# The gated short convolution of layer 1 moved into the slabs of its own input projection

## What is computed

```python
def short_conv_mix(h, conv_prefix, w_in, w_conv, w_out):
    gate_b, gate_c, xp = jnp.split(h @ w_in, 3, axis=-1)
    u = gate_c * xp
    u_ext = jnp.concatenate([conv_prefix.astype(u.dtype), u], axis=1)
    t = h.shape[1]
    y = w_conv[0] * u_ext[:, 0:t]
    for i in range(1, CONV_WIDTH):
        y = y + w_conv[i] * u_ext[:, i:i + t]
    return (gate_b * y) @ w_out, u_ext[:, -(CONV_WIDTH - 1):]
```

## Time and profile before

| | us |
|---|---|
| median of 3 runs | 3022.16 |
| lowest, highest run | 3018.03, 3022.17 |
| the profiled execution's own time | 3018.97 |
| its span (first to last instruction) | 3016.9 |
| PE busy in the span | 2865.7 (95%) |
| DVE, ACT, POOL busy | 1274.5, 860.5, 273.9 |

### The profile page before, as it was taken

How to read it: one execution, slowest core, us unless ns; L and a number is a source line. 1 busy time by engine, 2 the same in 40 slices (tenths; PEclk the granted TensorE clock), 3 DMA queues, 4 the chain that set the end, 5 groups by cost and what they waited for, 6 DMA issues and landing times.

```text
span 3016.9 us, 49528 instructions
## 1 busy us (share of the span) xinstructions
PE 2865.7 (95%) x21191; PEld 2776.5 (92%) x21191; DVE 1274.5 (42%) x1612; ACT 860.5 (29%) x891; POOL 273.9 (9%) x238
## 2 busy tenths in 40 slices
PE   6999999999996799999998689999999999999998
PEld 5987999999996799999998679999999878999997
DVE  3346543333435343334346654333343365433333
ACT  3136432222211232223223233122231264322222
POOL 5000100000104200000102620000010000000001
PEclk8999999999997899999999779999999999999999
DMA  3210232222221222222221012222222101322221
GB/s 122 87 65 1 80 109 82 84 84 84 84 84 42 56 84 84 84 84 70 85 70 64 1 42 84 84 84 84 81 96 77 53 32 60 113 84 84 84 84 46
DMA packets 205445, 223.38 MB, mean 74 GB/s; under 512 B 3734, under 2 KB 200416, under 8 KB 205312
## 3 DMA queue, kind: packets, MB, share of 16 engines
q1 hardware_dynamic: 200336, 203.70, 21.1%
q0 software_dynamic: 4976, 17.74, 1.8%
HBM read 208.56 MB, written 12.86 MB: 73 GB/s over the span
## 4 chain that ended last, share of the span: by engine, by line
PE 77%; issue 15%; DVE 3%; ACT 2%; POOL 2%; DMA 1%; POOLq 0%; DVEq 0%; ACTq 0%
PE bank L340 67%; PE bank L446 4%; PE bank L420 2%; PE bank L589 1%; POOL big L1420 1%; ACT big L795 1%; PE bank L477 1%; DMA out<-mixs 1%; PE bank L413 0%; PE bank L634 0%; DVE mixs L1128 0%; PE bank L631 0%; PE bank L643 0%; DVE stg L1221 0%; DVE stg L1248 0%
## 5 line engine op out<-in xcount | busy, mean ns | idle before, releaser
L340 PE MATMUL bank<-ahi,whi 128*128 128x288 f32 x3584 | 770.1, 297 | 7.0 <-DVE alo L1003 6.5
L340 PE MATMUL bank<-alo,whi 128*128 128x288 f32 x3584 | 767.4, 296 | 0.0
L340 PE MATMUL bank<-ahi,wlo 128*128 128x288 f32 x3584 | 767.1, 296 | 0.0
L682 ACT ACTIVATE whi<-raw 128x2048 fp32r<-128x2048 f32 x191 | 365.0, 1911 | 897.5 <-PE bank L340 877.6
L340 PE MATMUL bank<-hhi,whi 128*128 128x288 f32 x2560 | 556.6, 299 | 54.2 <-DVE hlo L1138 39.7
L340 PEld LDWEIGHTS bank<-ahi,whi 128*128 128x128 f32 x3584 | 578.5, 189 | 9.9 <-DVE wlo L976 7.4
L340 PEld LDWEIGHTS bank<-alo,whi 128*128 128x128 f32 x3584 | 578.2, 189 | 0.0
L340 PEld LDWEIGHTS bank<-ahi,wlo 128*128 128x128 f32 x3584 | 577.9, 189 | 0.0
L340 PE MATMUL bank<-hlo,whi 128*128 128x288 f32 x2560 | 553.2, 298 | 0.0
L340 PE MATMUL bank<-hhi,wlo 128*128 128x288 f32 x2560 | 553.2, 298 | 0.0
L976 DVE TENSOR_TENSOR wlo<-raw,whi 128x2048 fp32r<-128x2048 f32 x192 | 440.2, 2293 | 261.5 <-ACT whi L682 259.5
(11 more groups left out here) (250 smaller groups left out, 1787.4 us busy)
## 6 DMA issues: line engine op xcount, KB each, us to landing
raw<-in_mlp_w_up SPq DMA_DIRECT2D x64, 1024.0 KB, 5.3
raw<-in_mlp_w_down SPq DMA_DIRECT2D x64, 1024.0 KB, 5.1
raw<-in_sb_w_qkv SPq DMA_DIRECT2D x24, 1024.0 KB, 5.2
raw<-in_conv_w_in SPq DMA_DIRECT2D x12, 1024.0 KB, 5.2
raw<-in_gla_w_in SPq DMA_DIRECT2D x12, 1024.0 KB, 5.3
raw<-in_sb_w_o SPq DMA_DIRECT2D x8, 1024.0 KB, 5.3
out<-mixs POOLq DMA_DIRECT2D x3, 2048.0 KB, 7.7
out<-big POOLq DMA_DIRECT2D x2, 2048.0 KB, 8.4
```

The costliest lines, as they stand in the source:

```text
L340: mm = pe.matmul(acc[h][:, 0:HALF], w[:, u, k, m * P:(m + 1) * P], a[:, k, h * HALF:(h + 1) * HALF], start=(k == 0 and w is whi and a is a ...
L682: act.activation(whi[:, 1 - u], raw[:, 1 - u], ACT.Copy).then_inc(w_hi, 1)
```

## The change

Four things change, all in layer 1.

The order of the slabs. `in_chunk` and SP's loads take them in groups of three: columns of gate_c, then of xp, then of gate_b, for two chunks of channels at a time. So slabs 0, 1, 2 give chunks 8, 9, then 16, 17, then 0, 1 of `big`; four such groups make the 12 slabs.

The place of the convolution. GpSimd makes u of chunk c as soon as its xp chunk has been evacuated (slab 3i + 1). VectorE makes the taps of the even chunk behind slab 3i + 1, those of the odd one behind chunk m = 0 of slab 3i + 2 (`taps`), and the product with gate_b itself, in place in `big`, behind each chunk of slab 3i + 2. ScalarE's copy follows, and `lo_part` a chunk later, the last one at once. The third tap is written as two instructions (512 and 64 frames) over the xp chunk.

The buffers. `U` becomes two tiles of 580 frames in `e2` (made larger), `Y` one tile `conv_y`; `Gt` is gone. GpSimd copies the last two frames of each u to a new tile `tails`, which the four stores read after the last chunk. The two prefixes of the sample are copied chunk by chunk.

The wait of ScalarE for the four stores is gone. `run` has its slabs of layer 1 written out instead of looped on ScalarE and VectorE.

```diff
@@ -111,7 +111,9 @@
         rt, rt_m, rt_l = (sb(n, [P, NT], F32) for n in ("rt", "rt_m", "rt_l"))
-        e2 = sb("e2", [P, D], F32)
+        e2 = sb("e2", [P, 2 * 580], F32)
+        conv_y = sb("conv_y", [P, 578], F32)
+        tails = sb("tails", [P, 2, 2, KC], F32)
         split_r = passing("split_r", [P, 4 * D], F32R)
@@ -234,10 +236,8 @@
-        U = mixs[:, 0:KC * 580].rearrange("p (c t) -> p c t", c=KC)
-        Y = [mixs[:, 4640 + 580 * i:4640 + 580 * i + 578] for i in range(2)]
-        Gt = [mixs[:, 5800 + 576 * i:5800 + 576 * i + 576] for i in range(2)]
+        U = [e2[:, 580 * i:580 * i + 580] for i in range(2)]
+        prompt, sample = slice(0, TP), slice(TP, T)
@@ -276,6 +276,8 @@
+            if layer == 1:
+                return (8, 16, 0)[s % 3] + 2 * (s // 3) + m
             return (2 * s + m + 16) % 24 if layer == 2 else 2 * s + m
@@ -301,6 +303,11 @@
                     load(base + OUT_SLABS, mix_in[layer][:, :, 0:2 * D], IN_SLABS - OUT_SLABS)
+                elif layer == 1:
+                    for s in range(IN_SLABS):
+                        col = P * in_chunk(layer, s, 0)
+                        sp.wait_ge(w_lo, base + s + 1)
+                        sp.dma_start(raw[:, s % 2], mix_in[layer][:, :, col:col + SLAB]).then_inc(slab_in[s % 2], 16)
                 else:
@@ -827,11 +834,11 @@
-            def convolution(layer):
-                for c in range(KC):
+            def convolution(s, m):
+                if s % 3 == 2:
+                    c = 2 * (s // 3) + m
                     act.wait_ge(g_ready, c + 1)
-                    act.activation(hhi[:, c, :], Gt[c % 2], ACT.Copy).then_inc(mix_hi, 1)
-                act.wait_ge(stored, 16 * 4)
+                    act.activation(hhi[:, c, :], big[:, c, :], ACT.Copy).then_inc(mix_hi, 1)
@@ -917,9 +924,12 @@
                 base = first_slab(layer)
-                run(base, IN_SLABS, nothing, norm=2 * layer, beside=linear_gates if layer == 2 else None)
-                (stick_breaking if layer in (0, 3) else convolution if layer == 1 else linear_attention)(
-                    *((layer, layer // 3) if layer in (0, 3) else (layer,)))
+                run(base, IN_SLABS, nothing, norm=2 * layer, beside=linear_gates if layer == 2 else None,
+                    between=convolution if layer == 1 else None)
+                if layer in (0, 3):
+                    stick_breaking(layer, layer // 3)
+                elif layer == 2:
+                    linear_attention(layer)
@@ -1118,20 +1128,35 @@
-            def convolution(layer):
-                for c in range(KC):
-                    y = Y[c % 2]
-                    w = [vec[:, V_CONV + 8 * i + c:V_CONV + 8 * i + c + 1] for i in range(3)]
-                    dve.wait_ge(u_ready, c + 1)
-                    if c >= 2:
-                        dve.wait_ge(g_ready, c - 1)
-                    dve.tensor_scalar(y, U[:, c, 0:578], w[0], None, ALU.mult).then_inc(y_ready, 1)
-                    for i in (1, 2):
-                        dve.wait_ge(y_ready, 3 * c + i)
-                        dve.scalar_tensor_tensor(y, U[:, c, i:578 + i], w[i], y, ALU.mult, ALU.add).then_inc(y_ready, 1)
-                    if c:
-                        lo_part(layer, c - 1, Gt[(c - 1) % 2])
-                lo_part(layer, KC - 1, Gt[(KC - 1) % 2])
+            def taps(c):
+                w = [vec[:, V_CONV + 8 * i + c:V_CONV + 8 * i + c + 1] for i in range(3)]
+                u, y = U[c % 2], big[:, 16 + c, :]
+                dve.wait_ge(u_ready, c + 1)
+                dve.tensor_scalar(conv_y[:], u[:, 0:578], w[0], None, ALU.mult).then_inc(y_ready, 1)
+                dve.wait_ge(y_ready, 3 * c + 1)
+                dve.scalar_tensor_tensor(conv_y[:], u[:, 1:579], w[1], conv_y[:], ALU.mult, ALU.add).then_inc(y_ready, 1)
+                dve.wait_ge(y_ready, 3 * c + 2)
+                dve.scalar_tensor_tensor(y[:, prompt], u[:, 2:514], w[2], conv_y[:, 0:TP], ALU.mult, ALU.add)
+                dve.scalar_tensor_tensor(y[:, sample], u[:, 516:580], w[2], conv_y[:, 514:578], ALU.mult,
+                                         ALU.add).then_inc(y_ready, 1)
+            def convolution(s, m):
+                c = 2 * (s // 3) + m
+                if s % 3 == 0 and s and m == 0:
+                    lo_part(1, c - 1, big[:, c - 1, :])
+                elif s % 3 == 1 and m == 1:
+                    taps(c - 1)
+                elif s % 3 == 2:
+                    dve.wait_ge(acc_free, 2 * (first_slab(1) + s) + m + 5)
+                    dve.wait_ge(y_ready, 3 * c + 3)
+                    dve.tensor_tensor(big[:, c, :], big[:, c, :], big[:, 16 + c, :], ALU.mult).then_inc(g_ready, 1)
+                    if m == 0:
+                        taps(c + 1)
+                    else:
+                        lo_part(1, c - 1, big[:, c - 1, :])
+                    if c == KC - 1:
+                        lo_part(1, c, big[:, c, :])
@@ -1299,12 +1324,10 @@
                 run(base, IN_SLABS, project_out(layer), norm=2 * layer, beside=linear_gates if layer == 2 else None,
-                    unrolled=layer in (0, 3))
+                    between=convolution if layer == 1 else None, unrolled=layer in (0, 3))
                 if layer in (0, 3):
                     stick_breaking(layer, layer // 3)
-                elif layer == 1:
-                    convolution(layer)
-                else:
+                elif layer == 2:
                     linear_attention(layer)
@@ -1450,35 +1473,29 @@
                 pool.dma_start(sb_k_p[sb_index, 0].rearrange("(t p) h d -> p t (h d)", p=P), KT).then_inc(kv_stored, 16)
-                pool.dma_start(sb_k_s[sb_index, 0].rearrange("p h d -> p (h d)"), e2[0:TS, :]).then_inc(kv_stored, 16)
+                pool.dma_start(sb_k_s[sb_index, 0].rearrange("p h d -> p (h d)"), e2[0:TS, 0:D]).then_inc(kv_stored, 16)
             def convolution(layer):
-                pool.wait_ge(chunk_done, 2 * (first_slab(layer) + IN_SLABS) + 3)
-                pool.memset(U[:, :, 0:2], 0.0)
-                made(pool.tensor_copy(U[:, :, 514:516],
-                                      vec[:, V_STATE:V_STATE + 16].rearrange("p (i c) -> p c i", i=2)))
-                pool.wait_ge(acc_free, 2 * (first_slab(layer) + IN_SLABS) + 4)
-                def gate(c):
-                    g, y = Gt[c % 2], Y[c % 2]
-                    pool.wait_ge(y_ready, 3 * c + 3)
+                state = vec[:, V_STATE:V_STATE + 16].rearrange("p (i c) -> p c i", i=2)
+                pool.wait_ge(kv_stored, 16 * 4)
+                for i in range(2):
+                    made(pool.memset(U[i][:, 0:2], 0.0))
+                for c in range(KC):
+                    u = U[c % 2]
+                    pool.wait_ge(acc_free, 2 * (first_slab(layer) + 3 * (c // 2) + 1) + c % 2 + 5)
                     if c >= 2:
-                        pool.wait_ge(mix_ready, 8 * layer + c - 1)
-                    pool.tensor_tensor(g[:, 0:TP], y[:, 0:TP], big[:, c, 0:TP], ALU.mult)
-                    pool.tensor_tensor(g[:, TP:T], y[:, 514:578], big[:, c, TP:T], ALU.mult).then_inc(g_ready, 1)
-                for c in range(KC):
-                    pool.tensor_tensor(U[:, c, 2:514], big[:, 8 + c, 0:TP], big[:, 16 + c, 0:TP], ALU.mult)
-                    pool.tensor_tensor(U[:, c, 516:580], big[:, 8 + c, TP:T], big[:, 16 + c, TP:T],
+                        pool.wait_ge(y_ready, 3 * (c - 1))
+                    pool.tensor_copy(u[:, 514:516], state[:, c, :])
+                    pool.tensor_tensor(u[:, 2:514], big[:, 8 + c, prompt], big[:, 16 + c, prompt], ALU.mult)
+                    pool.tensor_tensor(u[:, 516:580], big[:, 8 + c, sample], big[:, 16 + c, sample],
                                        ALU.mult).then_inc(u_ready, 1)
-                    if c:
-                        gate(c - 1)
-                gate(KC - 1)
-                pool.wait_ge(u_ready, KC)
+                    pool.wait_ge(u_ready, c + 1)
+                    pool.tensor_copy(tails[:, 0, :, c], u[:, 512:514])
+                    made(pool.tensor_copy(tails[:, 1, :, c], u[:, 578:580]))
                 for i in range(2):
-                    for dst, at_ in ((conv_p, 512), (conv_s, 578)):
+                    for j, dst in ((0, conv_p), (1, conv_s)):
                         pool.dma_start(dst[0, 0, i].rearrange("(c p) -> p c", p=P).unsqueeze(2),
-                                       U[:, :, at_ + i:at_ + i + 1], allow_slow_non_contiguous=True).then_inc(stored, 16)
+                                       tails[:, j, i, :].unsqueeze(2), allow_slow_non_contiguous=True).then_inc(stored, 16)
```

More of the change, by code:

```diff
@@ L209, in weighted @@
         def weighted(u):
-            e = stg[:, (u + 1) * D:(u + 2) * D] if u < 3 else e2[:, :] if u % 5 == 4 else scr[:, u % 5 * D:(u % 5 + 1) * D]
+            e = stg[:, (u + 1) * D:(u + 2) * D] if u < 3 else e2[:, 0:D] if u % 5 == 4 else scr[:, u % 5 * D:(u % 5 + 1) * D]
```

## The result

| kernel | median us | runs, us | against before, 95% interval |
|---|---|---|---|
| before | 3021.33 | 3018.03 to 3022.17 (4) | |
| changed | 2975.06 | 2968.80 to 2976.70 (4) | 0.9851 (0.9838 to 0.9863) |

The change makes the kernel 1.5% faster, 46.3 us. The forecast was 2966.5 us, 55.54 us of gain, and the range ended at 2972: the direction was right, the time lies outside the range, and 8.6 us of the forecast median are missing.

The account below looks back on a forecast made before the run. TensorE's matmuls were taken to bound layer 1 except between input and output projection. Four terms there sum to 55.54 us; 3022.16 - 55.54 = 2966.6, rounded to 2966.5 us, range 2961 to 2972.

Parts of the forecast that it names:

- the four terms of the gain: Layer 1's turn to output projection: 10.83 us before the first matmul, 27.90 starved chunks, 14.54 behind stores, 2.27 slow start.
- the cover in the input projection: VectorE's added convolution work fits beside TensorE: 19.7 to 26.6 us of each 38.40 us group, costing zero.
- The rival of the port: Input projection: GpSimd holds VectorE up and TensorE stops, 0 to 12 us, most likely 4, giving 2970.6; chance 0.10.
- the tail: After the last input chunk: final `hlo` at about 3.6 us, needed at 5.6; cost zero, range 0 to 1.4 us.
- nobody waits for them until the end of the kernel: GpSimd's four stores (3.60 us of issuing) land beside the last slab and output projection, with no one waiting.
- one pace: TensorE's chunk of 48 matmuls costs 6.40 us wherever it runs unbroken, from 409.57 us for 64 chunks.

Follow-up runs that it names:

- the two traces at 6.24: The changed kernel with its four stores left out (median 2953.77 us), and with them written in pieces of 32 bytes (2960.44 us); layer 1 norm to norm 200.79 us in both.
- the second trace: The changed kernel profiled once more with no edit: median 2970.11 us, 0.9850 of before, layer 1 norm to norm 217.55 us.
- spread stores: The changed kernel with its four stores issued singly, two slabs apart, in layer 1's MLP: medians 2953.38 and, run again, 2950.67 us (0.9793 and 0.9775 of before).
- two stores: The changed kernel with two of its four stores left out: median 2964.09 us, 0.9815 of before, layer 1 norm to norm 206.23 us.

## Why the prediction was right and wrong

**Right: the four terms of the gain.** Waiting before the first matmul, starved chunks, ScalarE behind the stores, slow clock: all 55.54 us went. The two kernels that leave out nothing and only move the stores give 205.72 to 205.75 us in four traces against 205.76. That it fits to 0.04 us is in part luck: in these four traces layer 1 ran at 6.40 us a chunk, as the sum assumed; the two traces at 6.24 give 200.79.

**Right: the cover in the input projection, though the slow tap was another.** VectorE was busy 78.27 of 147.30 us, 20.4 per group of three slabs, near the least of the 19.7 to 26.6 forecast. With GpSimd at work the taps took 0.51, 1.88, 0.75 and 0.28 us, 3.4 in all against the 4.1 to 5.4 forecast. The first, which I took for the exposed one (1.53), was fast in all eight chunks; the second was slow in four of the eight, beyond the 1.28 I had as its dear value. With GpSimd idle they took 0.52, 0.82, 0.75 and 0.28. I had also misread one of the earlier trace rows: the tap of 0.52 us at 951.97 was not alone, a product of GpSimd began beside it at 952.13. It had only started first.

```profile
936.38 0.51 DVE L1136 TENSOR_SCALAR conv_y<-e,vec 128x578 f32<-128x578 f32 x1
936.93 1.88 DVE L1138 SCALAR_TENSOR_TENSOR conv_y<-e,vec,conv_y 128x578 f32<-128x578 f32 x1
938.84 0.75 DVE L1140 SCALAR_TENSOR_TENSOR big<-e,vec,conv_y 128x512 f32<-128x512 f32 x1
939.51 0.28 DVE L1141 SCALAR_TENSOR_TENSOR big<-e,vec,conv_y 128x64 f32<-128x64 f32 x1
939.70 2.28 DVE L986 TENSOR_TENSOR wlo<-raw,whi 128x2048 fp32r<-128x2048 f32 x1
942.04 0.82 DVE L1067 TENSOR_TENSOR big<-bank,rstd 128x288 f32<-128x288 f32 x2
...
949.30 0.76 DVE L1153 TENSOR_TENSOR big<-big 128x576 f32<-128x576 f32 x1
949.97 1.60 DVE L1163 TENSOR_TENSOR hlo<-big,hhi 128x576 fp32r<-128x576 f32 x2
```

The evacuation behind taps and split started at 942.04, 0.17 us after its chunk's end (941.87, one chunk before 948.27), which is no delay at all. The rival of the port cost nothing. The rule of the Trainium skill that the prediction cites ("SBUF — State Buffer", "Who interferes with whom") agrees with these rows: the first tap had ended when GpSimd's product began (936.89, 1.30 us), and the second, with two inputs in SBUF, began 0.04 us behind that product and took 1.88 us instead of 0.82.

**Right: the tail.** The last two `hlo` end at 951.57, 3.3 us after the last chunk (948.27, the evacuation's start less 0.17); 3.6 were forecast, and TensorE needed them at 5.6.

**Wrong: "nobody waits for them until the end of the kernel".** This is the step that failed. I moved the four stores from a place where no weight load was in flight (DMA share 0.06 in the earlier trace rows) to one just ahead of a load: GpSimd issues them at 940.13, SP the load of output slab 2 at 942.16. I looked for who waits for the stores, and found nobody. I did not ask what they slow down. The one sentence of the prediction on that load has it start later and has ScalarE read it a whole slab later still; it says nothing of the load's length, usually 5.2 us, and it was 32.8. The rows were there: 17.71 us until the last of four stores of 4 KB had landed meant that something else than bytes takes the time, and the kernel before hid that by standing still. The cost is the 6.08 us of idle and 34.11 - 32.00 = 2.11 us of slow clock after it, 8.19 in all, and 55.54 - 8.19 = 47.35 against the measured 47.37. In the second trace the same step costs 9.70 us of idle and 2.12 of slow clock. None of my rivals had a late load in it.

The Trainium skill ("DMA: Bandwidth & Descriptors", "Queues, rings and completion order") says that each DMA engine takes turns between its queues by whole packets. The trace shows that the two queues share, and not how: the engines moved some 25 GB/s in the middle of the collision, and over 300 where the load ran alone (GB/s in 40 slices, 940 to 985 us of the changed kernel, then 936 to 975 us of the one without stores).

```profile
GB/s 0 4 10 7 0 54 31 23 25 25 25 25 19 18 29 21 35 23 30 119 324 167 33 15 14 25 51 39 38 49 57 98 190 186 56 28 159 374 367 32
```

```profile
GB/s 0 0 0 0 21 309 379 337 29 0 0 0 0 0 0 0 17 68 294 377 299 36 1 0 0 0 0 0 0 0 99 209 381 355 32 0 0 0 0 0
```

The time shows up in the load's own packets: the packets of the same three loads took 62.5% of 45 us on 16 engines (450 us) in the changed kernel and 25.6% of 39 us (160 us) without stores, while the stores' own took 2.6% of the 45 (19 us). Whether a load's packet stands there waiting for its turn, and what a turn of 4-byte pieces lasts, no run here shows.

**Wrong as well: one pace.** "6.40 us wherever TensorE runs unbroken" came from the long stretches. The kernel before has one at 6.29 on average, layer 0's input projection (144.66 us for 23 chunks, against 147.19, with a granted clock of 0.95 in its first 21.6 us), and I had not looked at it. So the range was too narrow on the low side too: the kernels without the gap have medians of 2951 to 2966, and the forecast of 2966.5 would have stood at their upper edge even without the collision. The rival I held likeliest, VectorE held up by GpSimd, had its middle at 2970.6, near the measured time, for a wrong reason.

## What to carry to other kernels

When a wait for a transfer is removed or a transfer is moved, ask not only who waits for it but which transfers it will now share the DMA engines with, and price it by its pieces: 16 KB in pieces of 4 bytes delayed a 1 MB load by 28 to 31 us, 4 KB by 10. Send such a store where no load is needed soon, one at a time with room between, or make its runs longer where the layout allows it. And when the end of a chain is taken away, look up each resource that stood idle during it, since the next wait comes from what will now be busy there.

## What was not expected of the hardware

**TensorE has two paces at full clock.** Between two norms, where it runs unbroken, a chunk takes 6.40 us or 6.24 on average over the whole stretch, at a granted clock of 1.00 in both cases. The chains of the changed kernel and of the one with spread stores, for the same 64 chunks of layer 1's MLP:

```profile
1015.16 409.57 PE bank L347 x3072
```

```profile
1007.51 399.50 PE bank L347 x3072
```

That is 10 us on one MLP, 5 us on layer 1 (204.78 or 199.82 us for 32 chunks). Which pace a stretch gets changes between executions of the same kernel: layer 2's MLP was slow in the changed kernel's first profile (409.56) and fast in its second (399.50), layer 3's input projection fast in the first (143.67 for 23 chunks) and slow in the second (147.21). It is not wholly a lottery: layer 1's MLP was fast in both profiles with spread stores and slow in all others. What sets it stays open. Medians of such a kernel can differ by 10 us with no wait added or removed, and a stretch between two marks of the trace is the better measure.

**TensorE can pause without a semaphore beside such stores.** With the stores on ScalarE's queue, and in the kernel before without its wait, TensorE paused 0.6 to 3.3 us at a time in the middle of a chunk, released by nothing the profile shows. With two stores it was one pause of 0.28 us; with four stores on GpSimd's queue in the changed kernel, or with none, there is no such pause. Why is open.
